# Three seams of the third block: the first head's tiles, the second gates, and the sums of the final norm

## The reference, cut to what matters

```
h = rms_norm(x, g_pre)
u_a, v_a, z_a, q_b, k_b, v_b, z_b, gate_a, gate_b = split(h @ w_in)
y_a = spatial_gating(gelu(u_a), gelu(v_a), ...) * silu(z_a)
y_b = mixture_of_dilations(q_b, k_b, v_b) * silu(z_b)     # 8 heads of 128, dilations 1, 4, 16
m = sigmoid(gate_a + b) * (y_a @ w_pa) + sigmoid(gate_b + b') * (y_b @ w_pb)
return x + rms_norm(m @ w_o, g_post)
```

## Time and profile before

| what | us |
|---|---|
| runs | 4892.65, 4896.01, 4895.8 (median 4895.8) |
| the profiled execution, its own time | 4893.03 |
| its span (first to last instruction) | 4891.3 |
| PE busy | 4290.0 (88%) |
| DVE, ACT, POOL busy | 1865.1, 1334.0, 1087.4 |
| mean granted TensorE clock | 0.936 of 2.4 GHz |

### The profile page before, as it was taken

How to read it: one execution, slowest core, us unless ns; L and a number is a source line. 1 busy time by engine, 2 the same in 40 slices (tenths; PEclk the granted TensorE clock), 3 DMA queues, 4 the chain that set the end, 5 groups by cost and what they waited for, 6 DMA issues and landing times. The chain is left out here.

```text
span 4891.3 us, 55712 instructions
## 1 busy us (share of the span) xinstructions
PE 4290.0 (88%) x21602; PEld 3516.2 (72%) x21602; DVE 1865.1 (38%) x3257; ACT 1334.0 (27%) x2341; POOL 1087.4 (22%) x544
## 2 busy tenths in 40 slices
PE   8997888869983888569999999999899999956897
PEld 6886766657862877557888886888688888845775
DVE  3031565662575665224245234000133333345433
ACT  3120333342213444222000003112144443442121
POOL 2220001241231655211222222222011111122220
PEclk9997999969996999889999999999999999968898
DMA  3243102231323110211111112332323343265322
GB/s 119 101 146 80 33 14 48 76 95 35 139 95 132 38 40 18 84 49 43 48 48 52 44 43 81 115 134 93 92 82 99 105 106 90 79 207 165 138 85 79
DMA packets 277870, 412.02 MB, mean 84 GB/s; under 512 B 52853, under 2 KB 187894, under 8 KB 272122
## 3 DMA queue, kind: packets, MB, share of 16 engines
q1 hardware_dynamic: 206010, 298.36, 20.0%
q10 hardware_dynamic: 69424, 105.53, 6.0%
q0 software_dynamic: 2192, 4.80, 0.4%
HBM read 285.66 MB, written 122.95 MB: 84 GB/s over the span
## 5 line engine op out<-in xcount | busy, mean ns | idle before, releaser
L142 POOL TENSOR_TENSOR weights_wlow<-weights_raw,weights_whigh 128x1024 fp32r<-128x1024 f32 (+1 forms) x236 | 667.4, 2850 | 2529.8 <-ACT weights_whigh L133 2529.8
L275 PE MATMUL acc<-h_high_half,weights_whigh 128*128 128x512 f32 x1440 | 564.1, 392 | 77.3 <-POOL weights_wlow L142 76.1
L133 ACT ACTIVATE weights_whigh<-weights_raw 128x1024 fp32r<-128x1024 f32 (+1 forms) x236 | 266.2, 1162 | 1260.5 <-PE acc L275 812.4
L275 PE MATMUL acc<-h_high_half,weights_wlow 128*128 128x512 f32 x1440 | 563.1, 391 | 0.0
L275 PE MATMUL acc<-h_low_half,weights_whigh 128*128 128x512 f32 x1440 | 562.9, 391 | 0.0
L275 PEld LDWEIGHTS acc<-h_high_half,weights_whigh 128*128 128x128 f32 x1440 | 272.0, 189 | 136.3 <-POOL weights_wlow L142 77.7
L3174 PE MATMUL acc<-h_high_half,weights_whigh 128*128 128x512 f32 x768 | 332.6, 433 | 0.0
L275 PEld LDWEIGHTS acc<-h_high_half,weights_wlow 128*128 128x128 f32 x1440 | 272.1, 189 | 56.6
L275 PEld LDWEIGHTS acc<-h_low_half,weights_whigh 128*128 128x128 f32 x1440 | 271.8, 189 | 56.5
L3174 PE MATMUL acc<-h_low_half,weights_whigh 128*128 128x512 f32 x768 | 303.2, 395 | 0.0
L3174 PE MATMUL acc<-h_high_half,weights_wlow 128*128 128x512 f32 x768 | 302.0, 393 | 0.0
(11 more groups left out here) (522 smaller groups left out, 8089.3 us busy)
## 6 DMA issues: line engine op xcount, KB each, us to landing
weights_raw<-w_cols SPq DMA_DIRECT2D x94, 512.0 KB, 5.0
weights_raw<-w_ff SPq DMA_DIRECT2D x64, 512.0 KB, 3.8
weights_raw<-w_rows SPq DMA_DIRECT2D x30, 1024.0 KB, 7.1
att<-gated_result_sb SPq DMA_DIRECT2D x96, 130.0 KB, 2.1
rows<-norm_square ACTq DMA_DIRECT2D x48, 256.0 KB, 2.1
weights_raw<-w_out SPq DMA_DIRECT2D x24, 512.0 KB, 3.8
cols<-first_out ACTq DMA_DIRECT2D x40, 256.0 KB, 2.0
cols<-second_out ACTq DMA_DIRECT2D x32, 256.0 KB, 2.1
```

The costliest lines, as they stand in the source:

```text
L133: self.core.nc.scalar.activation(high[p][:, half * (KC // 2):(half + 1) * (KC // 2), :], raw[half], ACT.Copy).then_inc(self.core.sem("roun ...
L142: self.core.nc.gpsimd.tensor_tensor(low[p][:, hs, :], raw[half], high[p][:, hs, :].bitcast(F32), ALU.subtract).then_inc(self.core.sem("wei ...
L275: mm = nc.tensor.matmul(core.acc[b][:, :], wt[p][:, k, c * P:(c + 1) * P], h[:, k, half * HALF:(half + 1) * HALF], start=first, stop=final)
```

## The change

1. **First head ahead.** A new aside `FirstHead` on `rows3z` issues six of head 0's DMAs (q, k, `mid4`, two `end4`, `all16`, all into `x`) from SP, after all weight loads of that product. `scores(0)` waits for these six only. The `fetch` Block is gone: in the main Block SP issues, in this order, the slope, the four constants, `mid1` and two `end1`. DVE's first step waits for the constants and those four, PE's first `mix` for the four. For later heads the same ten DMAs are issued, q, k, `mid4` and `all16` (and `end4` of even heads) first.
2. **Second gates later.** For `proj_b` the eight gate DMAs move from the `scalar` hook to `emptied(it=0, b=1)`: on ACT after the eight L410 roundings and the rounding of block 1's weights.
3. **Final norm inside `proj_o`.** `norm_in_place` is replaced by `FinalNorm`, an aside of `proj_o`, in halves of 512 positions.

```diff
@@ dense: hooks
+    final = inner = aside if isinstance(aside, FinalNorm) else None
 POOL, after weights.rest(it):
+                if final: final.pool_after(pool, it)
 POOL, at the end:
+            if final: final.pool_last(pool)
 PE, in the loop over k of bank b:
+                        if inner and k % 4 == 0:
+                            inner.tensor_at(pe, it, b, k)
 PE and ACT, after all blocks:
+            if final: final.tensor_last(pe)
+            if final: final.scalar_last(a)
@@
+class FinalNorm:
+    ADDED_BY_POOL = (1, 3, 5)
+    EARLY = 6
+    def sync(self, sp, first):          # after all weight loads
+        if first: return
+        for k in range(KC): sp.dma_start(self.add_to[:, k, :], self.core.d["x3"][:, k, :]).then_inc(self.sig("residual"), 16)
+        ...                             # 16 stores of 128x512, h outer, k inner, each after its add
+    def square(self, a, k, h):          # ACT, 128x512
+        b = 2 * (k % 2) + h
+        a.wait_ge(self.core.sem(f"emptied_{b}"), self.at[b] + k // 2 + 1)
+        if k >= 2: a.wait_ge(self.sig("totalled"), k - 1)
+        self.core.nc.scalar.activation(self.squares[k % 2][:, self.half(h)], self.x[:, k, self.half(h)], ACT.Square)
+    def emptied(self, a, it, b):        # squares of the block before, after ACT rounded the next weights
+        if it and b == 3:
+            for k in (2 * it - 2, 2 * it - 1):
+                for h in range(2): self.square(a, k, h)
+    def scalar_last(self, a):
+        for h in range(2): self.square(a, KC - 2, h)
+        for h in range(2):
+            part = self.rstd[:, self.half(h)]
+            self.square(a, KC - 1, h)
+            a.wait_ge(self.sig("summed"), h + 1)
+            nc.scalar.activation(part, self.core.acc[4 + h][:, :], ACT.Ln, bias=self.core.eps[:, 0:1], scale=1.0 / D)
+            nc.scalar.activation(part, part, ACT.Exp, scale=-0.5)
+    def pool_after(self, pool, it):
+        for k in {2: (1,), 3: (2, 3)}.get(it, ()): self.add_squares(pool, k)    # total += squares, 128x1024
+    def pool_last(self, pool):
+        for k in (4, 5): self.add_squares(pool, k)
+        for h in range(2):
+            for k in self.ADDED_BY_POOL:
+                pool.wait_ge(self.sig("normed"), h * KC + k + 1)
+                ...                     # add_to half += x half, on POOL
+    def tensor_at(self, pe, it, b, k):
+        if (it, b, k) == (KC // 2 - 1, 3, 0):
+            pe.wait_ge(self.sig("totalled"), self.EARLY)
+            for h in range(2): self.sum(pe, self.total, h, True, False)         # ones x 128x512, float32
+            pe.wait_ge(self.sig("squared"), 2 * (KC - 1))
+            for h in range(2): self.sum(pe, self.squares[0], h, False, False)
+        if (it, b, k) == (KC // 2 - 1, 3, KC // 2):
+            pe.wait_ge(self.sig("squared"), 2 * KC - 1)
+            self.sum(pe, self.squares[1], 0, False, True)
+    def tensor_last(self, pe):
+        pe.wait_ge(self.sig("squared"), 2 * KC)
+        self.sum(pe, self.squares[1], 1, False, True)
+    def vector(self, v):                # after the 16 copies
+        for h in range(2):
+            v.wait_ge(self.sig("rstd"), h + 1)
+            for k in range(KC):
+                nc.vector.scalar_tensor_tensor(out=x, in0=x, scalar=self.g[:, k:k + 1], in1=self.rstd[:, hs], ...)
+                if k not in self.ADDED_BY_POOL:
+                    nc.vector.tensor_tensor(to, to, x, ALU.add)
@@
+class FirstHead:
+    def sync(self, sp, first):
+        if not first:
+            sp.wait_ge(self.core.sem("residual_stored"), 16)
+            for to, of in head_in_x(self.core.d, self.x, 0):
+                sp.dma_start(to, of).then_inc(self.core.sem("head_ahead"), 16)
@@ Gates
     def emptied(self, a, it, b):
-        pass
+        if self.later and it == 0 and b == 1:
+            self.load(a)
@@ gated_columns
-        fetch(core, att.constants)
@@ scores
-        if g % HEAD_SLOTS == 0:
-            pe.wait_ge(self.sig(f"head_loaded{it % 2}"), 16 * self.LOADS * (it // 2 + 1))
+        if g == 0:
+            pe.wait_ge(self.core.sem("head_ahead"), 96)
+        elif g % HEAD_SLOTS == 0:
+            self.wait_loaded(pe, it)
```

More of the change, by code:

```diff
@@ L175, in dense @@
     merge = aside if isinstance(aside, Merge) else None
+    final = aside if isinstance(aside, FinalNorm) else None
+    inner = aside if isinstance(aside, FinalNorm) else None
     arrived, at_arrived = [core.sem(f"arrived_{part}") for part in ("high", "low")], core.counts.of("arrived")
@@ L238, in rest_of_block @@
                     merge.pool_after(pool, it)
+                if final:
+                    final.pool_after(pool, it)
             if late:
@@ L244, in _ @@
                 weights.rest(pool, at, upcoming[2], blocks, blocks % 2)
+            if final:
+                final.pool_last(pool)
         @block.tensor
@@ L323, in _ @@
             over_blocks(pe, multiply)
+            if final:
+                final.tensor_last(pe)
         def empty_bank(eng, it, b):
@@ L427, in _ @@
                 merge.scalar_last(a)
+            if final:
+                final.scalar_last(a)
             if store:
@@ L693, in _ @@
                     nc.vector.tensor_tensor(low[:, k, :], at(k), high[:, k, :].bitcast(F32), ALU.subtract).then_inc(sig("split"), 1)
[L696 to L744, removed]
@@ L3001, in load @@
             sp.wait_ge(self.sig("mixed"), HEAD_SLOTS * (it - 1))
-        sp.dma_start(self.q[p], cols[QB + it * AE:QB + (it + 1) * AE, :]).then_inc(loaded, 16)
-        sp.dma_start(self.k[p], cols[KB + it * AE:KB + (it + 1) * AE, :]).then_inc(loaded, 16)
+        if it:
+            for to, of in head_in_x(d, self.x, it):
+                sp.dma_start(to, of).then_inc(loaded, 16)
         sp.dma_start(self.slope[p][:, :], d["dil_slope"][it, :, :]).then_inc(loaded, 16)
+        if it == 0:
+            for to, of in self.constants:
+                sp.dma_start(to, of).then_inc(self.sig("constants"), 16)
         sp.dma_start(self.mid1[p][:, :, :], v[BAND:SEQ - BAND, :].rearrange("(c p) e -> p c e", p=P)).then_inc(loaded, 16)
@@ L3077, in maxima @@
         v.wait_ge(self.sig("scores"), g + 1)
+        if g == 0:
+            v.wait_ge(self.sig("constants"), 16 * len(self.constants))
+            self.wait_loaded(v, 0)
         if g >= 2:
@@ L3422, with __init__ @@
 class Gates:
-    def __init__(self, core, tile, rows, also=None):
-        self.core, self.tile, self.rows, self.also = core, tile, rows, also
+    def __init__(self, core, tile, rows, also=None, later=False):
+        self.core, self.tile, self.rows, self.also, self.later = core, tile, rows, also, later
         self.first = core.counts.of("gates_in_0")
@@ L3432, in sync, with load @@
         pass
-    def scalar(self, a):
+    def load(self, a):
         for k in range(KC):
@@ L3439, in scalar @@
                 a.dma_start(self.also[0][:, k, :], self.also[1][k * P:(k + 1) * P, :]).then_inc(self.core.sem("yb_loaded"), 16)
+    def scalar(self, a):
+        if not self.later:
+            self.load(a)
     def emptied(self, a, it, b):
-        pass
+        if self.later and it == 0 and b == 1:
+            self.load(a)
     def vector(self, v):
@@ L3858, in bass_three_blocks_kernel @@
                 c3.close()
-                dense(core, "proj_o", y, d["w3_out"], 0, 4, 256, empty=write_columns(core, x), empties=1, weights=weights,
-                      source=lambda k: x[:, k, :])
-                norm_in_place(core, "post3", x, gain(G_POST), gates_in, d["out"])
+                with Stage(core, "post3") as st:
+                    dense(core, "proj_o", y, d["w3_out"], 0, 4, 256, empty=write_columns(core, x), empties=1, weights=weights,
+                          source=lambda k: x[:, k, :], aside=FinalNorm(core, st, x, gain(G_POST), gates_in))
 def _blocks(w, width):
```

105 lines of the change are left out of this document (98 added, 7 removed).

## The result

| | before | after |
|---|---|---|
| runs beside each other on one chip, us | 4891.27 to 4896.01, median 4894.23 (4) | 4851.47 to 4859.15, median 4858.08 (4) |
| profiled execution, its own time / span | 4893.03 / 4891.3 | 4857.09 / 4855.4 |
| mean granted clock | 0.936 | 0.938 |

The changed kernel is faster by 0.8%: ratio 0.9924, 95% interval 0.9907 to 0.9941, 36 us. The forecast was 4856 (4847 to 4864). Of the 35.9 us by which the span is shorter, PE's busy time makes 9.3 (4290.0 before), with 20 matmul instructions fewer, since the sums of squares take 12 now and took 32. The rest is time in which PE stood still, at a seam or behind its last matmul.

The account below looks back on a forecast made before the run. PE, busy for 88% of the span, or the tail behind it was taken to set the time. Gains of 17.1 + 5.8 + 15.9 = 38.8 us from 4893.0 give 4854.2, against the median 4857.0; forecast 4856 (4847 to 4864).

Parts of the forecast that it names:

- seam A: Between the end of `rows3z` and `turn(0)`, the first head: loading its tiles earlier gains 17.1 us (15.2 to 18.1).
- seam C: Final norm, from the last copy of `proj_o` to the span's end: moving it inside gains 15.9 us (10.5 to 23.9).
- The data term: First head: constants and value DMAs, the last issued at about 3492.1, land by 3495.1, so `turn(0)` goes at 3497.5.
- PE's side: First head: PE, starting at half clock, is ready for `turn(0)` between 3495.2 and 3498.3, middle 3496.8.
- Moving SP's wait: Entry of `rows3z`: SP waits there for the stores of `rows3v`; some 19 us of cover, so no cost.
- Seam B: Start of `proj_b`: ACT's eight gate issues leave the place before its first rounding, gaining 5.8 us (4.3 to 6.0).
- rival 4: Inside `proj_o`: adds or squares hold up weight rounding, PE loses up to a block at two blocks; 4900 us, chance 0.02.
- the stretch: After the last copy of `proj_o`: DVE's 26 multiplies and adds, 17.0 us, plus 7.6 for POOL's six adds: 24.6 us.
- the tail: From DVE's last step to the span's end: 3.2 us with half the bytes in the last store, 3.7 before.
- (1): Final norm: POOL's and DVE's adds do run side by side, 7.6 us more gain, time 4848; chance 0.12.
- (2): Final norm: turns between DVE and POOL cost more, with late stores some 5 us, time 4861; chance 0.12.
- (3): First head or gates: late DMA data is the bound, 5 to 7 us less gain, time 4862; chance 0.10.

Follow-up runs that it names:

- multiplies_first: The changed kernel with the norm's inverse roots in PSUM and, in each half, all eight multiplies before DVE's five adds: 4850.11 us (one run).

## Why the prediction was right, step by step

- **The sum, forecast 38.8, measured 35.9 between the two profiled executions and 36.2 between the medians.** At the seams it was 37.9; about 2 us were lost between them, most of it in a part of the block that spreads by more than that. The total came nearer than its terms did: seam A gave 2.0 us less than forecast and seam C 1.0 us more, and that these offset each other is luck.
- **The gains add up.** Shown at the seams by the three one-edit kernels: 37.8 us against 37.9. The medians (36.4 against 36.2) agree, within intervals too wide to show it alone.
- **Seam A, forecast 17.1 (15.2 to 18.1), measured 15.1, just under its range.** The mechanism held: `turn(0)` is set by the data, and the 2.48 us from DVE's start to `turn(0)` were forecast as 2.4. The data term was mis-sized. The last `end1` was issued 4.6 us after the Block's start, not 3.9, since the two `near_ends` issues alone took 2.11 us; and it took 4.3 us to reach DVE where I took 3.0, for transfers of 32 to 448 KB with nothing large ahead. The earlier trace rows had said 4.9, and I should have stayed nearer to it. The Block started 3.25 us after the product's end, as forecast (3.2). PE's side came out at its slow bound, 9.85 us from `scores(0)` (I expected 8.5): that cost nothing here, as the data was later still.
- **Moving SP's wait costs nothing.** Right: SP issued the raw loads of `rows3z` at 3402.20, POOL split them at 3409.13, and PE waited for no weights before the product's end.
- **Seam B, 5.8, measured 5.9.** The likeness of the start of `proj_o` carried it (25.95 us there, 25.92 here). No DVE instruction waited for a gate's DMA. How near it came is in part the execution's doing, since the seam without its edit varied by 1.9 us.
- **Seam C, 15.9, measured 16.9.** Its terms: sums on PE 4.34 (4.7 forecast); roots and table loads hidden, as said; no wait inside `proj_o` for squares or totals (rival 4 falls); the stretch 23.51 (24.6); the tail 3.64 (3.2). Two errors in the stretch offset: 26 instructions without a clash take 17.84 us, not 17.0 (+0.8; 26 x 0.65 is 16.9, which the prediction has as 17.0), and a clash with POOL costs 0.95 us, not POOL's whole 1.27 (-1.9 for six): the other 0.3 us of each POOL add cost DVE nothing. The tail did not shrink with the bytes of the last store: with 256 KB it is what it was with 512 KB.
- **Rivals 1 to 3.** (1), the adds run side by side: falls with the six adds of 1.64 us, and `multiplies_first` shows what would have been so: the stretch in that form is 16.80, close to the 17.0 given for it. (2), dearer turns, falls: each cost less. (3), the data as the bound at a seam: the forecast had the data as the later of the two at A already, and it came 2.0 us later than forecast, not 5 to 7.

What isn't settled: why `rows3z` ends anywhere between 3481 and 3491 us, and whether the first edit costs about 1 us behind `turn(0)`. The first spread is there without the change too (3481 to 3489) and is larger than seam B's gain; a gain of a few us here is read from a seam and not from one total.

## What to carry to other kernels

When an engine is given a share of another's elementwise work, look at what will run beside it: here six adds given to POOL, met by adds of DVE that read two SBUF tiles, cost 1.3 us more than keeping them on DVE; the same six beside multiplies with one operand in PSUM cost nothing, and the stretch fell from 22.22 to 16.80. When a start is brought forward, list all that the first dependent step waits for: PE could start 16 us earlier, but `turn(0)` came only 15, held by the last of eight DMAs that DVE's first step did not need yet. The three edits, at places where the same engine stands idle one after the other, added up here within what could be told, and each was best read at its own seam, in more than one execution.

## What the runs showed of the hardware

- After a short gap on PE the clock fell in most executions, but not in all. Behind the gap of 3.28 us at seam A the granted clock of the next 2 us was 0.50 in two of eight profiled executions, 0.55 to 0.58 in three and 1.00 in three; the four matmuls there took 1.62, 1.32 to 1.44 and 0.89 us. Behind the gap of 2.95 us at the starts of `proj_b` and `proj_o` the clock of the next 3.6 us was 0.50 to 0.69 in 17 of 19 cases. The two at 1.00 are of one execution, `multiplies_first`, which had kept full clock at seam A too. With matmuls in the gaps it was 1.00 in all six cases, which are of two executions: too few to call the matmuls the cause.
- A DVE add (two SBUF operands) that meets a POOL add takes 1.64 us instead of 0.69, and POOL's takes 1.64 to 1.71 instead of 1.26. A DVE multiply with one operand in PSUM neither waits for POOL's add nor holds it (0.67 and 1.24 us side by side). Six POOL memsets of 0.53 us, each beside a DVE multiply with two SBUF operands, delayed no DVE instruction. The Trainium skill, "SBUF — State Buffer", section "Who interferes with whom", states that a DVE instruction with two SBUF inputs contends with a GpSimd instruction that reads SBUF, and that the one issued second blocks until the first ends. The runs agree, with these prices.
- On ACT, Ln followed by Exp took a table load of 1.28 us for each (L769, L771), four in the norm.
